# Feed-forward up-projections by one level of Strassen's scheme

## The reference

```python
def swiglu(x, w_gu, w_down):          # x (512, 1024), w_gu (1024, 2*2816), w_down (2816, 1024)
    gate, up = jnp.split(x @ w_gu, 2, axis=-1)
    return (jax.nn.silu(gate) * up) @ w_down
# x = layer_norm(ALPHA * x + swiglu(...))
```

## Time and profile before

| | us |
|---|---|
| median of 3 runs | 2985.76 (2982.86 to 2991.48) |
| the profiled execution | 2982.55 |
| its span | 2980.7 |
| PE busy | 2905.9 (97%) |
| POOL busy | 1643.1 (55%) |
| DVE busy | 953.6 (32%) |
| ACT busy | 744.5 (25%) |

### The profile page before, as it was taken

One profiled execution on the slowest core, in us unless ns is written; L12 is line 12 of the kernel. 1 busy time (PEld: TensorE's weight loads), 2 busy tenths in 40 slices (PEclk: granted clock), 3 DMA queues, 4 the chain that ended last, 5 costly groups with the idle time before them and its releaser, 6 DMA issues.

```text
span 2980.7 us, 35596 instructions
## 1 busy us (share of the span) xinstructions
PE 2905.9 (97%) x14808; PEld 2418.5 (81%) x14808; DVE 953.6 (32%) x1443; ACT 744.5 (25%) x1492; POOL 1643.1 (55%) x1338
## 2 busy tenths in 40 slices
PE   8989999999999999999999999999999998999998
PEld 7877888888888768888888888788888886788887
DVE  3745414111035484141110333732110238521102
ACT  2236323101024363230100222532010233420001
POOL 5840472666657504726666467526666566166663
PEclk9999999999999999999999999999999998999999
DMA  4241331322223204213222333013222231132222
GB/s 144 95 136 49 127 113 57 102 97 99 99 96 110 71 15 141 99 63 108 99 99 91 101 99 99 1 43 113 95 91 98 99 106 57 40 112 91 98 99 85
DMA packets 184548, 271.21 MB, mean 91 GB/s; under 512 B 6708, under 2 KB 145972, under 8 KB 184388
## 3 DMA queue, kind: packets, MB, share of 16 engines
q1 hardware_dynamic: 174240, 243.28, 24.4%
q10 hardware_dynamic: 10148, 25.66, 2.6%
HBM read 266.79 MB, written 2.13 MB: 90 GB/s over the span
## 4 chain that ended last, share of the span: by engine, by line
PE 81%; DVE 8%; DMA 3%; POOL 3%; ACT 2%; issue 1%; ACTq 0%; DVEq 0%; POOLq 0%
PE PS L485 24%; PE PS L486 23%; PE PS L487 23%; POOL wlo L2437 3%; PE PS L913 3%; PE PS L575 2%; DVE a_qk L1341 2%; PE PS L883 1%; DVE nmx L1676 1%; PE PS L1069 1%; ACT whi L651 1%; PE PS L1527 1%; DVE d_a L1670 0%; PE PS L2376 0%; PE PS L2180 0%
## 5 line engine op out<-in xcount | busy, mean ns | idle before, releaser
L2437 POOL TENSOR_TENSOR wlo<-raw,whi 128x512 fp32r<-128x512 f32 x881 | 1170.0, 1360 | 542.3 <-ACT whi L651 542.3
L485 PE MATMUL PS<-xT_hi,whi 128*128 128x512 f32 (+1 forms) x2304 | 847.1, 368 | 12.7 <-DVE xT_lo L595 6.6
L486 PE MATMUL PS<-xT_lo,whi 128*128 128x512 f32 (+1 forms) x2304 | 842.6, 366 | 0.0
L487 PE MATMUL PS<-xT_hi,wlo 128*128 128x512 f32 (+1 forms) x2304 | 842.6, 366 | 0.0
L2429 POOL TENSOR_SCALAR whi<-raw 128x1024 fp32r<-128x1024 f32 x384 | 416.9, 1104 | 659.8 <-DMA raw<-ffn_w 225.8
L485 PEld LDWEIGHTS PS<-xT_hi,whi 128*128 128x128 f32 x2304 | 435.1, 189 | 88.0 <-DVE xT_lo L595 8.7
L486 PEld LDWEIGHTS PS<-xT_lo,whi 128*128 128x128 f32 x2304 | 435.2, 189 | 70.4 <-issue 1.0
L487 PEld LDWEIGHTS PS<-xT_hi,wlo 128*128 128x128 f32 x2304 | 435.1, 189 | 70.3
L1111 DVE TENSOR_TENSOR htmp<-sil,PS 128x512 f32<-128x512 f32 x88 | 56.5, 683 | 804.6 <-ACT sil L1096 804.6
L485 PE MATMUL PS<-whi,h_hi 128*128 128x512 f32 x704 | 274.8, 390 | 1.0 <-POOL wlo L2437 1.0
L487 PE MATMUL PS<-whi,h_lo 128*128 128x512 f32 x704 | 274.0, 389 | 0.0
(11 more groups left out here) (383 smaller groups left out, 3108.4 us busy)
## 6 DMA issues: line engine op xcount, KB each, us to landing
raw<-ffn_w SPq DMA_DIRECT2D x66, 1024.0 KB, 4.9
raw<-ffn_w_gu SPq DMA_DIRECT2D x44, 1024.0 KB, 5.0
raw<-ffn_w_down SPq DMA_DIRECT2D x22, 1024.0 KB, 4.8
raw<-mem_wkv SPq DMA_DIRECT2D x16, 1024.0 KB, 5.2
raw<-even_w_in SPq DMA_DIRECT2D x14, 1024.0 KB, 5.1
raw<-ev_w_in SPq DMA_DIRECT2D x14, 1024.0 KB, 5.1
raw<-odd_w_in SPq DMA_DIRECT2D x12, 1024.0 KB, 5.2
raw<-od_w_in SPq DMA_DIRECT2D x10, 1024.0 KB, 5.0
```

What stands on the lines that cost most here:

```text
L485: pe.matmul(o, lhs[0], rhs[0], start=start, stop=False, skip_group_check=True)
L486: pe.matmul(o, lhs[0], rhs[1], start=False, stop=False, skip_group_check=True)
L487: return pe.matmul(o, lhs[1], rhs[0], start=False, stop=stop, skip_group_check=True)
L2437: m = pool.tensor_tensor(wlo[b][:, cs], raw[b][:, cs], whi[b][:, cs].bitcast(F32), ALU.subtract)
```

## The change

In each feed-forward stage the first pair stays as it was. The other ten pairs become units. With k and tokens halved and B the (gate, up) blocks of 512 x 256, a unit forms the 2x2 block product by the Winograd form of Strassen's scheme, seven half products of 512 (k) x 256 (columns of W) x 256 (tokens):

- from the weights, on POOL, per unit: V1 = B12 - B11, V2 = B22 - V1, V4 = B21 - V2, B12' = B22 - B12 (each 128 x 1024), for the unit after the one that TensorE works on; V1 waits for that one's product 2, V2 for its product 3;
- from x, once per stage: x32 = hi + lo (three quarters on POOL, one on DVE), s1, s2, s4 (DVE), s3 (POOL), and their splits (ACT, DVE);
- each of the seven weight operands is split by ACT (hi, in a ring of four buffers) and DVE (lo, in place), each 128 x 1024, three products ahead. POOL's and ACT's panel cuts don't occur in units;
- products are summed in PSUM where the scheme allows, the rest by ACT's copy of P1 and five DVE additions (PSUM + SBUF, 128x512); two products a unit of silu and up go to POOL;
- the hidden tiles are stored whole (h_all) and split in hi and lo during the down-projection, two at a time, in four buffers;
- units' blocks are loaded by SP as four transfers of 0.5 MB into the panel slots, each when the product that used its place two units before is done; the first three down panels wait for products in place of panels.

The core of the diff (stage_ffn; places, counters and the hidden tiles' copies left out):

```diff
-                for i in range(FF // 256):
-                    cols(up, 256 * i, 256)
-                    cols(up, FF + 256 * i, 256)
-                    jobs.append(Job("GU", "dve", "gu", 2 * i))
+                cols(up, 0, 256)
+                cols(up, FF, 256)
+                jobs = [Job("GU", "dve", "gu", 0)]
...
+            def act(act, step):
+                def hi(q):
+                    u, k = divmod(q, 7)
...
+                    if k in (0, 3, 5):
+                        act.wait_ge(*loaded(u, {0: 0, 3: 2, 5: 3}[k]))
+                    else:
+                        act.wait_ge(t_done, 4 * g + {1: 1, 2: 2, 6: 3, 4: 4}[k])
+                    if q >= 4:
+                        act.wait_ge(u_prod, 7 * g0 + q - 3)
+                    act.activation(ring_hi[q % 4][1][:, :, :], source(u, k)[0][:, :, :], ACT.Copy).then_inc(b_hi, 1)
...
+                hi(0)
+                sum_to_hi(0)
+                hi(1)
+                sum_to_hi(1)
+                hi(2)
...
+                        if k == 4:
+                            act.wait_ge(u_prod, 7 * g + 4)
...
+                            act.activation(u_gate[:, :], PS[:, a_, :], ACT.Silu).then_inc(gate_ready, 1)
+                        if 7 * u + k + 3 < 7 * UNITS:
+                            hi(7 * u + k + 3)
+                        if k == 1 and u >= 1:
+                            act.wait_ge(evac_unit, 5 * g)
+                            act.activation(u_c21[:, :], u_c21[:, :], ACT.Silu).then_inc(sil2_ready, 1)
...
             def dve(dve, step):
+                dve.wait_ge(lo_ready, n_turn["dve"])
+                dve.tensor_tensor(x32[:, k_low, high], xT_hi[:, k_low, high].bitcast(F32), xT_lo[:, k_low, high].bitcast(F32),
+                                  ALU.add).then_inc(sums, 1)
...
+                dve.wait_ge(x_parts, 4 * f + 3)
...
+                dve.tensor_tensor(s1, x32[:, k_low, high], x32[:, k_high, high], ALU.add).then_inc(sums, 1)
...
+                dve.tensor_tensor(s2, s1, x32[:, k_low, low], ALU.subtract).then_inc(sums, 1)
...
+                dve.tensor_tensor(s4, s4, s2, ALU.subtract).then_inc(sums, 1)
+                lo(0)
+                sum_to_lo(0)
+                lo(1)
+                sum_to_lo(1)
+                lo(2)
...
+                for u in range(UNITS):
+                    for k in range(7):
+                        if k == 0 and u >= 1:
+                            gate2_part(u - 1)
+                        if k == 2:
+                            dve.wait_ge(u_prod, 7 * g + 2)
...
+                            dve.tensor_tensor(u_s5[:, :], PS[:, c_, :], u_s1[:, :], ALU.add).then_inc(evac_unit, 1)
+                        if k == 3:
+                            dve.wait_ge(u_prod, 7 * g + 3)
...
+                            dve.tensor_tensor(u_u2[:, :], PS[:, b_, :], u_s1[:, :], ALU.add).then_inc(evac_unit, 1)
+                        if k == 5:
+                            dve.wait_ge(u_prod, 7 * g + 5)
...
+                            dve.tensor_tensor(u_c22[:, :], PS[:, b_, :], u_s5[:, :], ALU.add).then_inc(evac_unit, 1)
+                        if k == 6:
+                            dve.wait_ge(u_prod, 7 * g + 6)
...
+                            dve.tensor_tensor(u_u2[:, :], PS[:, c_, :], u_u2[:, :], ALU.add).then_inc(evac_unit, 1)
+                        if 7 * u + k + 3 < 7 * UNITS:
+                            lo(7 * u + k + 3)
+                        if u == 0 and k in (1, 2):
+                            sum_to_lo(k + 1)
...
+            def pool(pool):
+                pool.wait_ge(lo_ready, turns_before[index] - NT + 2)
+                part(k_low, low)
+                part(k_high, low)
+                pool.wait_ge(lo_ready, turns_before[index])
+                part(k_high, high)
+                weight_sums(0)
+                pool.tensor_tensor(sum_lo[2][0][:, :, :], x32[:, k_low, low], x32[:, k_low, high], ALU.subtract).then_inc(x_parts, 1)
+                for u in range(UNITS):
+                    if u >= 1:
+                        hidden(pool, u - 1)
+                    if u + 1 < UNITS:
+                        weight_sums(u + 1)
...
+                        if k == 3:
+                            pe.wait_ge(s1_ready, g + 1)
+                        if k in (4, 5, 6):
+                            pe.wait_ge(evac_unit, 5 * g + (2, 1, 3)[k - 4])
+                        if u == 0 and k in (1, 2, 4, 5):
+                            pe.wait_ge(sums_lo, 4 * f + {1: 1, 2: 2, 4: 3, 5: 4}[k])
+                        pe.wait_ge(b_lo, 7 * g0 + q + 1)
+                        for c in range(2):
+                            cs = slice(128 * c, 128 * c + 128)
+                            for kk in range(4):
+                                m = product(pe, PS[:, bank, 256 * c:256 * c + 256], (h_[:, kk, cs], l_[:, kk, cs]),
+                                            (xh[:, kk, :], xl[:, kk, :]), k < 3 and c == 0 and kk == 0, kk == 3)
+                        m.then_inc(u_prod, 1)
```

More of the change, by code:

```diff
@@ L129, in build, with block @@
         w = Area("W")
[L130 to L134, removed]
+        h_all = w("h_all", [P, NF, S])
+        sums_at, temps_at, ring_at = w.off, w.off + 24576, w.off + 36864
+        ln_sq = place("ln_sq", "W", ring_at + 8192, [P, D])
+        def block(name, region, off):
+            return (place(name, region, off, [P, 4, 256]), place(name + "_r", region, off, [P, 4, 256], F32R))
+        sum_hi, sum_lo = ([block(f"sum_{n}{i}", "W", sums_at + 8192 * i + o) for i in range(3)]
+                          for n, o in (("hi", 0), ("lo", 4096)))
+        u_s1, u_u2, u_s5, u_c22, u_c21, u_gate = (place(f"u_{n}", "W", temps_at + 2048 * i, [P, 512])
+                                                  for i, n in enumerate(("s1", "u2", "s5", "c22", "c21", "gate")))
+        sil = place("sil", "W", temps_at + 8192, [P, 2, S])
+        ring_hi = [block(f"ring{i}", "W", ring_at + 4096 * i) for i in range(4)]
+        split_at = [(sums_at + 8192 * i, sums_at + 8192 * i + 4096) for i in range(3)] + [(ring_at, ring_at + 4096)]
+        hs_hi, hs_lo = ([place(f"hs_{n}{i}", "W", at_[j], [P, 2, S], F32R) for i, at_ in enumerate(split_at)]
+                        for j, n in enumerate(("hi", "lo")))
+        raw_block = [[block(f"rawb{i}{j}", "raw", 4 * PANEL * i + 4096 * j) for j in range(2)] for i in range(NB)]
+        hi_block = [[block(f"hib{i}{j}", "hi", 4 * PANEL * i + 4096 * j) for j in range(2)] for i in range(NB)]
+        in_h = [block(f"in_h{i}", "W", 2048 * i) for i in (8, 10, 12)]
+        x32 = place("x32", "W", 2048 * 14, [P, KD, S])
         w = Area("W")
@@ L699, in pe_block_out @@
                 add(1, 2)
[L700 removed]
+            three += last_three(2)
             finish(0)
@@ L1080, in stage_cross @@
                     "head": {"pe": head_pe, "act": head_act, "dve": head_dve}}
+        UNITS = NF // 2 - 1
+        unit_loads = {}
+        raw_wait = {}
+        hi_wait = {}
         def stage_ffn(st, jobs):
-            n0 = counts.get("ffn_tiles", 0)
-            count("ffn_tiles", NF)
-            sil_ready, h_ready, hhi_ready = S_("silu_ready"), S_("hidden_ready"), S_("hidden_hi_ready")
-            def act(act, step):
[L1088 to L1100, removed]
@@ L1102, in dve @@
-            def dve(dve, step):
[L1103 to L1118, removed]
+            f = stage_no["ffn"]
@@ new lines, in stage_ffn @@
+            stage_no["ffn"] += 1
+            g0 = UNITS * f
+            index = program.index((st, jobs))
+            n0 = last_panel[index] - NF // 2 - 1
+            d0 = n0 + 2
+            sa, sb, sc = n0 % NB, (n0 + 1) % NB, (n0 + 2) % NB
+            pair = jobs[0]
+            u_prod, t_done, b_hi, b_lo, s1_ready, evac_unit, gate_ready, sil2_ready, h_done, x_parts, sums, sums_hi, sums_lo,\
+                split_hi, split_lo, sil_ready = (S_(n) for n in (
+                    "unit_product", "unit_sums", "block_hi", "block_lo", "unit_p1", "unit_evacuated", "unit_gate", "unit_gate2",
+                    "unit_hidden", "x_parts", "x_sums", "x_sums_hi", "x_sums_lo", "hidden_hi", "hidden_lo", "silu_ready"))
@@ new lines, in hidden @@
+            def hidden(pool, u):
+                g = g0 + u
+                tiles = h_all[:, 2 * u + 2:2 * u + 4, :]
+                halves = lambda ap: ap.rearrange("p (c n) -> p c n", c=2)
+                pool.wait_ge(gate_ready, g + 1)
+                pool.wait_ge(evac_unit, 5 * g + 4)
+                pool.tensor_tensor(tiles[:, :, low], halves(u_gate[:, :]), halves(u_u2[:, :]), ALU.mult).then_inc(h_done, 1)
+                pool.wait_ge(sil2_ready, g + 1)
+                pool.wait_ge(evac_unit, 5 * g + 3)
+                pool.tensor_tensor(tiles[:, :, high], halves(u_c21[:, :]), halves(u_c22[:, :]), ALU.mult).then_inc(h_done, 1)
@@ L1120, in pe @@
             def pe(pe):
                 pe_split(pe, jobs, 1)
-                pe_projections(pe, rest(jobs))
```

(40 more changed lines are left out.)

184 lines of the change are left out of this document (175 added, 9 removed).

## The result

| | before | after |
|---|---|---|
| median, us | 2985.49 (4 runs) | 3015.99 (3013.55 to 3019.17, 4 runs) |
| ratio | | 1.0098, 95% interval 1.0079 to 1.0117 |
| span of the profiled execution | 2980.7 | 3011.6 |
| granted clock, mean | 0.993 | 0.983 |

A forecast was written before the change was run, and what follows sets the result against it. The prediction took TensorE, busy 97% of the span, as the bound. From 2982.6 us it counted -65 (columns), +68 (stage starts) and +13 (steady waits) to 2998 us; range 2930 to 3035, the forecast's own 2985 to 3015.

The forecast's parts named there:

- Fewer columns: TensorE in the feed-forward units: 168 half-width matmuls take 20.13 us against 21.76, 1.63 us won per unit, 65 us in all.
- The start of a stage: First unit of each feed-forward stage: TensorE waits while DVE and POOL alternate, 17 us lost per stage, 68 for four.
- the even odds that s1 wins its turn from V1: At a stage's start: DVE's s1 might go before POOL's V1, saving 3.5 us; even odds, so 17 us was taken.
- The steady wait: Seventh product of later units waits for DVE's c22: 0.7 us, none in the next unit; 0.37 per unit, 13 us.
- The slow clock: After TensorE's long waits at a stage's start, matmuls run at half speed: some 1.5 us more per stage.
- Rival 1: Stage starts: the cover holds because alternation is cheaper (port shared within an instruction, or DVE wins turns); 2952 or 2917 us, chance 0.33.
- Rival 2: Feed-forward units: POOL becomes the bound of every unit, 21.6 us each, 54 us in place of 13, about 3040; chance 0.12.
- the forecast's load of 19.4 us of 20.1: POOL in each unit: 12.5 us of work plus 7 x 0.98 us held back by DVE; it holds, barely.
- Moved elsewhere: Hidden-tile splits, panel cuts and loads moved to the down-projection and change over: hidden behind other work, no cost.

The follow-up runs named there:

- c_halves: Changed kernel with each of POOL's four weight sums issued as two 128x512 instructions instead of one 128x1024: 2975.65 us, 0.9978 of the kernel before.
- a_c22: Changed kernel with the addition c22 moved ahead of the lo subtraction before it in DVE's queue in every unit: 2993.16 us, 1.0028 of the kernel before.

## Why the prediction was right and wrong

- **Fewer columns, 65 us won.** Right: units without waits take 20.16 us (forecast 20.13), 1.60 won each, 64 us. The price of a half-width matmul was read from the split first pair.
- **The start of a stage, 17 us: right in mechanism and place, too low in size.** The chain of turns was worked out as 3.48 us per turn, measured 3.35; the first product began at 544.64 (forecast 545.4), u2 ended at 567.4 (forecast 569). (The forecast's four turns from 553.0 make 566.9 and not the 566.1 that it wrote; that slip of 0.8 us is inside its error.) The loss is 18.3 us in the first stage and 18.6 in the mean, 74 us in place of 68. What failed is the even odds that s1 wins its turn from V1, with which 19.4 was brought down to 17: in all four stages V1 goes first. POOL runs on from its own part of x32 into V1 (531.13), while s1 has to wait for that part and begins 0.14 us later.
- **The steady wait, 0.37 per unit: the term that was mis-sized most.** Forecast was 0.7 in one unit and none in the next, "with POOL shifted by it". The size of one wait was right; that every second unit has none is the step that failed. Measured: 0.65 in every unit but a stage's first and last, 32 x 0.65 = 21 us in place of 13. DVE and POOL in one unit (c22 is L1311):

```profile
626.80 3.36 DVE L1242 TENSOR_TENSOR rawb_r<-rawb,ring_r 128x1024 fp32r<-128x1024 f32 x1 [0.46 <-ACT ring_r L1175]
630.09 0.68 DVE L1304 TENSOR_TENSOR u_u<-PS,u_s 128x512 f32<-128x512 f32 x1
630.69 2.83 DVE L1242 TENSOR_TENSOR hib_r<-hib,ring_r 128x1024 fp32r<-128x1024 f32 x1
633.44 3.42 DVE L1242 TENSOR_TENSOR rawb_r<-rawb,ring_r 128x1024 fp32r<-128x1024 f32 x1
636.79 0.68 DVE L1311 TENSOR_TENSOR u_c<-PS,u_s 128x512 f32<-128x512 f32 x1
```

```profile
620.13 2.15 POOL L1333 TENSOR_TENSOR h_all<-u_gate,u_u 128x512 f32<-128x512 f32 x1 [1.83 <-DVE u_u L1315]
624.91 1.82 POOL L1336 TENSOR_TENSOR h_all<-u_c,u_c 128x512 f32<-128x512 f32 x1 [2.63 <-ACT u_c L1229]
626.69 2.39 POOL L1352 TENSOR_TENSOR hib<-hib,rawb 128x1024 f32<-128x1024 f32 x1
```

```profile
636.85 0.28 PE L500 MATMUL PS<-xT_hi,rawb_r 128*128 128x256 f32 x1
637.52 0.39 PE L498 MATMUL PS<-xT_hi,ring_r 128*128 128x256 f32 x1 [0.40 <-DVE u_c L1311]
637.75 0.28 PE L499 MATMUL PS<-xT_lo,ring_r 128*128 128x256 f32 x1
```

  POOL's row begins anew in each unit with ACT's second silu, which hangs on TensorE's product. So when TensorE waits, POOL moves with it and nothing shifts between them: V1 begins at 626.69, 0.1 us before DVE asks at 626.80, and in 31 of the 32 units that wait it is 0.11 or 0.12 us. Each of the three subtractions above is held in its turn, and c22 comes too late behind them. That the tie to the silu is what keeps the two in step is argued from these rows; no run cut it. TensorE's rows give the price: from 636.85 to 637.52 the starts are 0.67 us apart and not 0.12 (0.55 lost), and the matmul after is followed by the next 0.22 us on (0.10 lost), 0.65 in all. The 0.40 of the profile counts from the end of a matmul's record, 0.28 us behind its start.
- **The slow clock, 1.5 us per stage.** Right: seen after both waits. The fifth product began 16.7 us late (567.50, against 539.32 + 4 x 2.88 = 550.8), and of the 18.3 us lost 1.6 are left for the clock behind it. The first wait's slow matmuls were covered, as forecast: they ended at 549.0, when the second block had just been split (549.02).
- **The sum**: -64 + 74 + 21 = +31, spans +30.9. The forecast: -65 + 68 + 13 = +16. Of the 15 us between them 8 are the steady wait, 6 the start and 1 the columns. Rival 1, the same turns at a lower price, fails by the start loss itself, 18.6 us where it needed under 13, and its port shared within an instruction by c_halves and by the 1.08 us. Rival 2, POOL full, fails by the units' 20.8 us, by a_c22, where the same work in another order loses nothing, and by POOL's idle time, 1.83 + 2.63 us in each unit; the forecast's load of 19.4 us of 20.1 was 3 us too high, since not every DVE subtraction meets a POOL instruction. "Moved elsewhere": nothing, as forecast.

## What to carry to other kernels

Where two helper engines took turns, as DVE and POOL did here, their work was to be added up and not laid side by side, and each wait counted in whole instructions of the other engine. Two cures worked. Order alone (the short addition that TensorE waits for ahead of long subtractions, u2 and the first sums earlier, POOL held back) gave 77 us, more than the scheme itself wins (64). Short instructions on POOL alone gave 40 and, on top of the order, nothing measurable. A steady loss shows best as the period of a unit. Before a forecast lets a wait average out over units, look at what starts the other engine's row: here it hung on TensorE's own product, and the wait came back in every unit. Before a stage starts, look for what could be made in a helper's idle time: three edits of order turned 1.0% slower into 1.6% faster.

## What the hardware showed that I had not expected

- A POOL memset of 128x1024 (0.96 us) does not hold up a DVE instruction with two SBUF inputs (1.23 us beside it); a POOL instruction that reads does (3.3 us). The Trainium skill (SBUF — State Buffer, Who interferes with whom) says so of instructions that only write, and the trace agrees.
- A wait that the profile gives as 0.40 us costs TensorE 0.65: 0.55 between the starts on its two sides, and 0.10 more before the next matmul.
- A turn costs less than the sum of both: 3.35 us for 1.22 + 2.39, so some 0.25 us of each pair overlap; with POOL's 128x512 it is the same (2.23 for 1.22 + 1.255).
